# A query group's sigmoid, a rank product, an expert's list and the last norm moved in a hybrid mixer and expert layer

## The reference

```python
def hg_dir(p, z, lb):                      # the gated recurrence of a head
    q = jax.nn.silu(to_heads(p[4], HG_HEADS))
    f = lbh + (1.0 - lbh) * jax.nn.sigmoid(to_heads(z, HG_HEADS))
    return q, 1.0 - f, to_heads(p[7], HG_HEADS), jnp.log(f)
...
h_lat = h_lat + g1[:, None] * y_x          # y_x: both head groups through w_out
v_x = rms_norm(h_lat, norm_ffn_w[l]) * (1.0 + sc2[:, None]) + sh2[:, None]
logits = (h @ router_w + router_b)
top_logit, top_idx = lax.top_k(logits, TOP_K)      # 4 of 32 experts
order = jnp.argsort(flat_e)                # tokens grouped by expert
...                                        # each expert: clamped SwiGLU
h_lat = h_lat + g2[:, None] * y
return rms_norm(h_lat, norm_final_w)
```

## Time and profile before

| | us |
|---|---|
| median of 3 runs | 2986.96 |
| lowest and highest | 2986.31, 2991.73 |
| the profiled execution | 2993.08 |
| its span, first to last instruction | 2991.4 |
| TensorE busy (share of the span) | 2723.6 (91%) |
| VectorE busy | 2022.6 (68%) |
| ScalarE busy | 1439.3 (48%) |
| mean granted TensorE clock | 0.948 |

### The profile page before, as it was taken

The page is one execution under the profiler, slowest core; times in us unless marked ns, Lnnn a source line. Parts: engine busy times, 40 slices in busy tenths (PEclk is TensorE's granted clock), DMA queues, the critical chain, the costliest instruction groups (busy, mean ns, idle before and its releaser), DMA issues. The chain is left out here.

```text
span 2991.4 us, 38797 instructions
## 1 busy us (share of the span) xinstructions
PE 2723.6 (91%) x13213; PEld 2190.3 (73%) x13214; DVE 2022.6 (68%) x2183; ACT 1439.3 (48%) x1464; POOL 502.1 (17%) x437
## 2 busy tenths in 40 slices
PE   6988989849868859999999999999999999999993
PEld 6575866738667747877777787878878877787772
DVE  5266656552066669699987969676676677967874
ACT  3144343332163447477755747454454455645552
POOL 0045332320001311021111102020111111111110
PEclk7799999969979979999999999999999999999996
DMA  8301010010114389599987959586576688958863
GB/s 350 128 28 29 22 29 15 8 64 29 50 43 134 110 288 357 196 354 356 357 292 255 364 193 359 185 300 204 185 270 201 203 278 284 352 197 277 284 216 133
DMA packets 263801, 596.68 MB, mean 199 GB/s; under 512 B 21086, under 2 KB 46342, under 8 KB 260562
## 3 DMA queue, kind: packets, MB, share of 16 engines
q1 hardware_dynamic: 243348, 552.56, 51.5%
q0 software_dynamic: 20384, 43.19, 6.5%
HBM read 577.75 MB, written 42.25 MB: 207 GB/s over the span
## 5 line engine op out<-in xcount | busy, mean ns | idle before, releaser
L1942 DVE TENSOR_TENSOR e_slot_r<-e_slot,whi 128x2048 fp32r<-128x2048 f32 x296 | 674.6, 2286 | 128.8 <-ACT whi L1882 128.8
L1882 ACT ACTIVATE whi<-e_slot 128x2048 fp32r<-128x2048 f32 x296 | 561.1, 1912 | 376.1 <-PE e_acc L1793 376.1
L1793 PE MATMUL e_acc<-whi,e_xlo 128*128 128x512 f32 x1600 | 634.5, 397 | 0.0
L1791 PE MATMUL e_acc<-whi,e_xhi 128*128 128x512 f32 x1600 | 633.6, 396 | 0.5
L1882 ACT ACTIVATE whi<-slot 128x2048 fp32r<-128x2048 f32 x148 | 283.0, 1912 | 189.5 <-PE e_acc L1793 189.5
L1942 DVE TENSOR_TENSOR slot_r<-slot,whi 128x2048 fp32r<-128x2048 f32 x151 | 345.2, 2288 | 20.6 <-ACT whi L1882 17.8
L1793 PEld LDWEIGHTS e_acc<-whi,e_xlo 128*128 128x128 f32 x1600 | 300.2, 188 | 73.3
L1791 PEld LDWEIGHTS e_acc<-whi,e_xhi 128*128 128x128 f32 x1600 | 301.1, 188 | 66.3 <-DVE e_slot_r L1942 4.0
L1791 PE MATMUL e_acc<-whi,e_ahi 128*128 128x512 f32 x800 | 322.1, 403 | 0.0
L1793 PE MATMUL e_acc<-whi,e_alo 128*128 128x512 f32 x800 | 316.5, 396 | 0.0
L1792 PE MATMUL e_acc<-slot_r,e_xhi 128*128 128x512 f32 x800 | 313.0, 391 | 0.0
(11 more groups left out here) (292 smaller groups left out, 3927.5 us busy)
## 6 DMA issues: line engine op xcount, KB each, us to landing
e_slot<-in_w SPq DMA_DIRECT2D x296, 1024.0 KB, 6.9
slot<-in_w SPq DMA_DIRECT2D x151, 1024.0 KB, 6.2
slot<-in_w_ada SPq DMA_DIRECT2D x24, 1024.0 KB, 7.1
slot<-in_w_in SPq DMA_DIRECT2D x20, 512.0 KB, 4.0
slot<-in_w_in SPq DMA_DIRECT2D x6, 1024.0 KB, 7.9
xt<-in_x SPq DMA_DIRECT2D x8, 512.0 KB, 8.6
slot<-in_w_out SPq DMA_DIRECT2D x4, 1024.0 KB, 13.1
o_x<-in_x SPq DMA_DIRECT2D x8, 512.0 KB, 6.0
```

Of the source, the lines that this page charges most:

```text
L1791: pe.matmul(out, hi[:, k, c], wh, start=False, stop=False)
L1793: return pe.matmul(out, lo[:, k, c], wh, start=False, stop=last)
L1882: act.activation(whi[i % RING][:], raw[i % PIECES][:], ACT.Copy).then_inc(S["whi_made"], 1)
L1942: v.tensor_tensor(wlo[i % PIECES][:], raw[i % PIECES][:], whi[i % RING][:].bitcast(F32), ALU.subtract).then_inc(S["wlo_made"], 1)
```

## The change

Four separate edits.

1. **hgrn2.** `query_sig(h+1, 0)` moves on ScalarE from behind `decays(h+1)` to ahead of `roots(h, 1)`, right behind `logs(h+1)`. VectorE's `queries` is split by group: the first group's multiply now stands behind `keys(h+1)` and ahead of `finish(h, 1)`, the second stays.
2. **route.** `places(i-2)` is issued in the middle of `project_out(i)`, and no longer behind it.
3. **route and experts.** The first unit is always expert 0, whose list starts at address 0, so its load is issued at the end of `route`, by GpSimd, once the scatters have landed; its tile and semaphore now outlive the stage. VectorE makes the indices first and clears the gathering tiles after it.
4. **finish.** The norm's weights are loaded in `experts` by SyncE, into the weight slot that piece 3 of the last unit left. ScalarE takes each tile's root right behind its square, with scale and epsilon in the activation itself; VectorE's 8 small operations are gone.

```diff
@@ ScalarE and VectorE, hgrn2
                     logs(h + 1)
+                    query_sig(h + 1, 0)
                 if now:
                     roots(h, 1)
                 if more:
                     decays(h + 1)
-                    query_sig(h + 1, 0)
                     query_sig(h + 1, 1)
...
                     keys(h + 1)
+                    queries(h + 1, 0)
                 if now:
                     finish(h, 1)
                 if more:
                     decayed(h + 1, 0)
                     decayed(h + 1, 1)
-                    queries(h + 1)
+                    queries(h + 1, 1)
@@ TensorE, route
                 for k in range(KT):
+                    if k == KT // 2 and i >= 2:
+                        places(i - 2)
...
-                if i >= 2:
-                    places(i - 2)
                 if i >= 1:
                     logits(i - 1)
@@ GpSimd, end of route
             g.wait_ge(S["scattered"], 16 * TOPK * LT)
+            g.dma_start(keep["lists"][:], dram["lists"][0:CAP, :].rearrange("(b p) c -> p b c", p=P)).then_inc(keep["lists_in"], 16)
@@ experts: SyncE, GpSimd, VectorE
+            sp.wait_ge(S["piece_done"], before_last * PIECES + RING)
+            alone(sp, S["s_passed"])
+            sp.dma_start(raw[3][:, 0:D], dram["norm_final_w"]....to_broadcast((P, D))).then_inc(keep["nw_in"], 16)
...
-            load_lists(0)
             g.wait_ge(S["next_ready"], 1)
             g.wait_ge(S["set"], NB)
...
-            for x in xg:
-                v.memset(x[:], 0.0).then_inc(S["set"], 1)
...
+            next_index(16)
+            for x in xg:
+                v.memset(x[:], 0.0).then_inc(S["set"], 1)
             pick(0)
             rest(0, 0)
-            next_index(16)
@@ finish: ScalarE, VectorE
                 act.activation(sq[:], x[:, i, :], ACT.Square, accum_out=ms[:, i:i + 1]).then_inc(squared, 1)
-            for i in range(LT):
-                act.wait_ge(ms_ready, i + 1)
-                act.activation(ms[:, i:i + 1], ms[:, i:i + 1], ACT.Sqrt).then_inc(root_ready, 1)
+                act.wait_ge(squared, i + 1)
+                act.activation(ms[:, i:i + 1], ms[:, i:i + 1], ACT.Sqrt, scale=1.0 / D, bias=eps[:]).then_inc(root_ready, 1)
...
-                v.tensor_scalar(r, r, 1.0 / D, EPS, ALU.mult, ALU.add).then_inc(ms_ready, 1)
```

More of the change, by code:

```diff
@@ L735, in keys, with queries @@
                     v.tensor_scalar(key[h % 2][d][:], key[h % 2][d][:], bound[:, h, d, 2:3], bound[:, h, d, 1:2], ALU.mult, ALU.add).then_inc(S["keys_ready"], 1)
-            def queries(h):
-                for j in range(2):
-                    v.wait_ge(S["q_sig"], 2 * h + j + 1)
-                    at = slice(j * 512, (j + 1) * 512)
-                    v.tensor_tensor(q[h % 2][:, at], bank(h, 6 + j)[:], q[h % 2][:, at], ALU.mult).then_inc(S["q_ready"], 1)
+            def queries(h, j):
+                v.wait_ge(S["q_sig"], 2 * h + j + 1)
+                at = slice(j * 512, (j + 1) * 512)
+                v.tensor_tensor(q[h % 2][:, at], bank(h, 6 + j)[:], q[h % 2][:, at], ALU.mult).then_inc(S["q_ready"], 1)
             def decayed(h, n):
@@ L1629, in experts @@
         w_in = keep["w_in"]
+        lists, lists_in = keep["lists"], keep["lists_in"]
         xhi, xlo = t.sb("e_xhi", [P, KT, CAP], F32R), t.sb("e_xlo", [P, KT, CAP], F32R)
@@ L1636, in experts @@
         spark = t.sb("e_spark", [1, 1])
-        lists = t.sb("e_lists", [P, NB, 2])
         idx_next = t.sb("e_idx_next", [P, NB], U32)
@@ L1642, in experts @@
         tb = [t.ps(f"e_tb{i}") for i in range(2)]
-        names = """const_in set lists_in mid_ready next_ready now_ready pick_ready gates_ready whi_made wlo_made
+        names = """const_in set mid_ready next_ready now_ready pick_ready gates_ready whi_made wlo_made
         piece_done glu_ready lin_ready mix_ready sig_made act_ready turned hi_made lo_made y_taken scattered
@@ L1691, in _ @@
                 load_piece(sp, dram, keep, raw[i], i, bass.ds(e1, 1))
+            sp.wait_ge(S["piece_done"], before_last * PIECES + RING)
+            alone(sp, S["s_passed"])
+            sp.dma_start(raw[3][:, 0:D], dram["norm_final_w"].rearrange("(a n) -> a n", a=1).to_broadcast((P, D))).then_inc(keep["nw_in"], 16)
             for i in range(RING - 1):
@@ L1700, in load_lists @@
                 at = g.value_load(U[0:1, bass.ds(u + 3 * UNITS, 1)], min_val=0, max_val=NE * SEQ - CAP)
-                g.dma_start(lists[:], dram["lists"][bass.ds(at, CAP), :].rearrange("(b p) c -> p b c", p=P)).then_inc(S["lists_in"], 16)
+                g.dma_start(lists[:], dram["lists"][bass.ds(at, CAP), :].rearrange("(b p) c -> p b c", p=P)).then_inc(lists_in, 16)
             def gather(b):
@@ L1944, in next_index @@
             def next_index(loads):
-                v.wait_ge(S["lists_in"], loads)
+                v.wait_ge(lists_in, loads)
                 v.tensor_copy(idx_next[:], lists[:, :, 0]).then_inc(S["next_ready"], 1)
@@ L2049, in finish @@
         sq = t.sb("f_sq", [P, D])
-        nw = t.sb("f_nw", [P, D])
         ms = t.sb("f_ms", [P, LT])
-        w_in, squared, ms_ready, root_ready, inv_ready, ready, out = (t.sem("f_" + n) for n in ("w_in", "squared", "ms_ready", "root_ready", "inv_ready", "ready", "out"))
+        eps = t.sb("f_eps", [P, 1])
+        nw = keep["slots"][3][:, 0:D]
+        eps_set, squared, root_ready, inv_ready, ready, out = (t.sem("f_" + n) for n in ("eps_set", "squared", "root_ready", "inv_ready", "ready", "out"))
         x_in = [t.sem(f"f_x_in{i}") for i in range(LT)]
@@ L2067, in _ @@
         def _(act):
+            act.wait_ge(eps_set, 1)
             for i in range(LT):
@@ L2072, in _ @@
                 act.activation(sq[:], x[:, i, :], ACT.Square, accum_out=ms[:, i:i + 1]).then_inc(squared, 1)
-            for i in range(LT):
-                act.wait_ge(ms_ready, i + 1)
-                act.activation(ms[:, i:i + 1], ms[:, i:i + 1], ACT.Sqrt).then_inc(root_ready, 1)
+                act.wait_ge(squared, i + 1)
+                act.activation(ms[:, i:i + 1], ms[:, i:i + 1], ACT.Sqrt, scale=1.0 / D, bias=eps[:]).then_inc(root_ready, 1)
         @block.vector
         def _(v):
-            v.wait_ge(w_in, 16)
-            for i in range(LT):
-                r = ms[:, i:i + 1]
-                v.wait_ge(squared, i + 1)
-                v.tensor_scalar(r, r, 1.0 / D, EPS, ALU.mult, ALU.add).then_inc(ms_ready, 1)
+            v.memset(eps[:], EPS).then_inc(eps_set, 1)
+            v.wait_ge(keep["nw_in"], 16)
             for i in range(LT):
@@ L2088, in _ @@
                 v.wait_ge(inv_ready, i + 1)
-                v.scalar_tensor_tensor(x[:, i, :], x[:, i, :], r, nw[:], ALU.mult, ALU.mult).then_inc(ready, 1)
+                v.scalar_tensor_tensor(x[:, i, :], x[:, i, :], r, nw, ALU.mult, ALU.mult).then_inc(ready, 1)
 IN = ["x", "c", "ctx", "c_ctx", "w_ada", "b_ada", "norm_mix_w", "norm_ffn_w", "w_in", "w_out", "hg_lb",
@@ L2109, in build @@
             lb=m.sb("lb", [P, 8]), oml=m.sb("oml", [P, 8]), lb_ready=m.sem("lb_ready"), emptied=m.sem("emptied"), bound_part=m.sem("bound_part"), u_ready=m.sem("u_ready"), w_out_in=[m.sem(f"w_out_in{i}") for i in range(SLOTS)], hg_in=m.sem("hg_in"),
-            w_in=[m.sem(f"w_in{i}") for i in range(PIECES)],
+            w_in=[m.sem(f"w_in{i}") for i in range(PIECES)], nw_in=m.sem("nw_in"),
         )
@@ L2121, in build @@
         keep["own"] = m.sb("own", [P, UNITS])
+        keep["lists"], keep["lists_in"] = m.sb("list_now", [P, CAP // P, 2]), m.sem("lists_in")
         with ExitStack() as mix:
```

1 line of the change is left out of this document (removed).

## The result

| | before | changed |
|---|---|---|
| median, us | 2988.96 (4 runs) | 2955.31 (4 runs) |
| lowest and highest | 2986.31, 2991.73 | 2952.59, 2957.87 |
| profiled execution: span | 2991.4 | 2953.9 |

The ratio is 0.9887, with a 95% interval of 0.9873 to 0.9901: 33.7 us faster by the medians, 29.6 to 38.0 by the interval. The forecast was 2947.8 with a range to 2957: the range holds, the centre was 7.5 us too low.

What follows compares the result with a forecast made beforehand. TensorE, busy nearly throughout the experts stage, was taken as constant, so gains come from the 1115 us around it: 27.2 + 1.6 + 3.3 + 7.1 = 39.2 off the 2986.96 median gives 2947.8 us, range 2942 to 2957.

Steps and rivals of the forecast that it cites:

- Edit 1, waits: hgrn2: TensorE's waits for the query multiply vanish in heads 1 to 3, 14.7 us; head 0 restarts 5.0 us earlier.
- The cover: hgrn2, heads 1 to 3: second query group ready 1.9 us before TensorE needs it; extra table loads fit idle time.
- R3: hgrn2: the wait moves on inside a head, half of 22.2 us in heads 1 to 3 lost, 2958.9; chance 0.06.
- R4: hgrn2: the extra table loads are on the path, 5.1 us lost, 2952.9; chance 0.03.
- R6: hgrn2: first values still wait until the second group's multiply ends, 27.2 us lost, 2975.0; chance 0.01.
- R5: Expert loop: lower mean clock cancels the gain at 0.97, 2994.8 at 0.965; chance 0.02, 0.01 more near 0.97.
- Edit 1, clock: hgrn2, heads 1 to 3: without idle time the 64 first values run at the upper clock level, 7.5 us.
- R1: hgrn2: TensorE's clock falls behind the removed waits all the same, 7.5 us lost, 2955.3; chance 0.10.
- Edit 2: End of route: last residual starts about 0.4 us behind TensorE's end; 1.6 us, bounds 0 and 3.15.
- Edit 3: Route to expert loop: list asked for earlier, so the gather comes 3.3 us earlier; bounds named up to 6.1.
- R2: Route ends only when the list has landed, so 3.3 us shrinks to 0.3, 2950.8; chance 0.14.
- Edit 4: Finish: stores stand behind loads on the DMA engines, end at 2984.3 in place of 2991.4; 7.1 us, bounds 5 and 10.

Runs made afterwards that it cites:

- hg_act_only: Kernel before with only ScalarE's sigmoid of the first query group moved, VectorE's multiply left in place: early key product to projections 533.5 us, before 542.6.
- head0_first: Changed kernel with VectorE's first query multiply ahead of the keys before head 0: early key product to projections 515.6 us, changed kernel 516.2.
- list_sp_b: Changed kernel with SyncE instead of GpSimd asking for the list: from its issue to the meeting's release 3.96 us in place of 4.81.
- all_better: Changed kernel with list_sp_b, head0_first and each first gather waiting only for its own cleared tile: ratio 0.9864 to the kernel before, changed kernel beside it 0.9862.
- hg_only: Kernel before with edit 1 alone (first query group's sigmoid and multiply moved): ratio 0.9918, 24.5 us faster.
- stores_held: Changed kernel with the first store in finish issued only when all 8 loads have landed: load issue to end 25.3 us, changed kernel 25.2.

## Why the prediction was right, and where it missed

**Edit 1, waits: right.** 14.7 forecast and gone to the last digit; head 0's restart forecast at 168.0 against a trace of 168.25 that started 0.4 us later. The cover held: no wait for the second query group in heads 1 to 3, no table load on the path, VectorE in time. R3 and R4 fall, R6 too, and R5 with the expert loop at 1875.2 us.

**Edit 1, clock: right by the place, a little too large in sum.** Behind the waits the full 7.5 came (2.78, 3.03, 1.71) and 0.8 in head 0. What was not foreseen is the return: a fall at the first query groups, 1.7 us in head 1 and in head 2. Head 3, where such a fall stood before as well, gave 1.3 us that nobody had counted, in that group and just ahead of it. So the sum is 14.7 + 5.1 + 7.5 + 0.8 - 3.4 + 1.3, and 0.5 because a group without a wait overlaps the one ahead of it by 0.16 us, three times: 26.4 against 27.2, close by terms that cancel. Over the traces it is between 22.6 and 27.2. R1 is false as it was put, since the first values ran at full speed in heads 1 to 3 of all nine traces with edit 1, and true in part of the sum: between nothing and 4.6 us are lost again at other places. That a wait of 3 us is enough for a fall behind it, and that the fall behind it goes with the wait, is shown by hg_act_only beside the nine traces with edit 1. That a wait taken away in one place must show in the time is refuted by head0_first, where TensorE then waits for GpSimd's chain.

**Edit 2: right in kind, 1.6 forecast, 1.1 measured.** The residual did start 1.8 us earlier behind the last product (0.04 us behind its end in place of 1.88). But the two pairs of `places` products now lie ahead of that product's end, which the working left out. They are also more than the 0.30 us of the working: that row is the first pair alone, and together they moved the last product's end by 0.7 us.

**Edit 3: right in sum, partly by luck.** 3.3 forecast; 3.5 from the last scatter to the gather in the first pair of traces, 2.9 by the means, and about 3 at TensorE's first turned rows. The list could be asked for 3.14 us behind the last scatter (3.05 were assumed), but 3.9 to 5.3 us behind it in the other six traces where GpSimd asks. The forecast also expected the index to wait for the list, 8.75 us behind the last scatter, and the meeting to stay at 6.2. Instead the list was there before the meeting, and the meeting itself came at 7.95, which breaks the sign that the prediction gave for it. The two errors nearly cancel. R2 is refuted in its price, since the meeting moved by 1.8 us and not by the list's 5.7, and in its mechanism by the landings in list_sp_b and all_better. Of the 1.8 us 0.85 are the issue on GpSimd; the rest stays open.

**Edit 4: 7.1 forecast, 5.7 to 5.9 measured.** Terms of the sum were wrong in both directions. The 381 GB/s of the stores were read as the DMA engines' pace; they were VectorE's, one tile of 0.52 MB in 1.39 us, which is 377 GB/s. Stores that are not held back ran at 406 to 418, so 11.0 us should have been 10.0 to 10.3. And loads and stores were taken to follow one another, with a rule of the Trainium skill beside it ("DMA: Bandwidth & Descriptors", "Two DMAs through the same engine are not ordered", that descriptors start in order within one queue). The trace agrees for most of the bytes: the last of the loads, all issued before the first store, is there at 2943.4, 14.6 us behind the first issue, and 13.2 us where the stores are held. By then the changed kernel has moved about 4.9 MB, 4.2 of loads and 0.7 of stores (14.64 us at the 335 GB/s of the window below, of finish up to that point). So some stores are through before the last load is, which a rule on the order of starts does not exclude. What the sum lacked is the cost of the mixture, 1.1 us by the estimate above, and the thin end: behind 2951.9 only some 0.1 MB is moved, and the span ends at 2953.9, 2.0 us where the sum had 0.9.

```profile
2928.76:2943.40 14.64, 0.00 (x0) 0.00 (x0) 8.30 (x13) 10.84 (x22) 0.00 (x0) 0.50 0.92 335
```

**The step that missed most is the last one: setting the traced gain against the median.** The forecast is 7.5 us too low. 1.7 of them are the terms above: the traces give 37.5 against the forecast's 39.2. 2.0 are the base, which was the median of three executions, 2986.96, and became 2988.96 with the fourth. The other 3.8 are the distance from the pair of traces to the pair of medians: the kernel before has its median 4.1 below its profiled execution, the changed kernel 0.3 below its own. Between the two traces of before, 6.1 of the 7.3 us lie in the first stage, in which TensorE's clock gives 109.4 to 118.5 us to the same code. For the medians that cause is likely and not shown, since their executions have no traces. Had the forecast been left at the profiled execution (2993.08 - 39.2 = 2953.9), it would have been 1.4 from the median that came; that would have been luck in part, since both profiled executions had a long first stage. By the spread of the executions of one kernel, some 4 us is my estimate of the error of such a forecast with few runs, and that should have been in the range from the start.

## What to carry to other kernels

A wait on TensorE can cost more than its length: the matmuls behind it ran up to 3 us longer for 64 of them. Take that from rows with and without the wait, and allow for a fall of the clock at another place in its stead. Before a wait's length is counted as gain, follow the engines that TensorE waits for next: in head 0 a chain through GpSimd, untouched by the edit, took 4.3 of 4.6 us back. A bandwidth read in a stretch is the DMA engines' only if no other engine paces the transfers: divide the bytes of a transfer by the pitch of the engine that feeds it. Before a predicted gain is set against a median, compare two traces of the same kernel stage by stage, and see which stage makes the scatter.

## What the runs showed of the hardware

- The same stage, the same code, 9 us apart: between 60 and 70 us, in the first stage, the granted clock is 0.50 in one execution (50 matmuls) and 0.75 on the mean in another (71). In the traces of hg_only, stores_held and head0_first it is written as 1.00 while TensorE does 49 matmuls in 10 us, the pace that the others show at 0.50; there the record can't be taken at its word, and the matmuls' pitch decides.
- A clock fall has no fixed place. With waits of 4.9 and 3.06 us ahead of the first values the products behind the wait were slow every time (9.0 to 10.3 us for 64, in heads 1 to 3 of four traces). With no wait they took 7.31 us in heads 1 to 3 of nine traces, and a fall stood at the first query group instead (8.5 to 9.4 us for 16 products in place of 7.03): in head 1 in six of the nine, in heads 2 and 3 in all.
- An indirect DMA's landing varies: from the end of the last scatter's issue to the request that waits for it are 3.1 to 5.3 us in the nine traces that have such a request.
- A request for a list by GpSimd holds the stage's meeting up by 0.85 us against the same request by SyncE (from the issue to the release of VectorE 4.79 to 4.81 us in seven traces, 3.96 and 3.97 in two).
- The table load before the moved sigmoid took 1.28 us, and the activation started 1.30 behind the load's start, as in the earlier trace rows (ScalarE before head 0 of the changed kernel):

```profile
157.06 1.28 ACT L610 ACT_TABLE_LOAD   x1
158.36 0.60 ACT L610 ACTIVATE slot<-h_pj 128x512 f32<-128x512 f32 x1
```

The 2.7 us that the Trainium skill gives for a switch ("ScalarE: Activation LUTs", "Table sets: the hidden batching unit") show in no trace here.
